# Thirteen chunks of the second layer's modulation, for the x stream alone, from TensorE in the first FFN pass to VectorE beside the mLSTM's projections

## The chip, the cores and the metric

One core of a Trainium2 chip runs the whole program. The metric is the device time of one execution in microseconds; lower is better. The kernel before took 2405.74 us (median of three runs, 2401.69 to 2405.82).

## What is computed

A two-layer block on an x stream of 1024 tokens (16 rows of 64) and a context stream of 256 tokens, 1024 features, all in float32. Per layer and stream a modulation vector of 6 x 1024 values is made from a conditioning vector, and used as shift, scale and gate:

```python
m = jax.nn.silu(cond) @ w + b            # w is 1024 x 6144
sh1, sc1, gt1, sh2, sc2, gt2 = split(m)
hx = rms_norm(x, g0) * (1 + sc1) + sh1   # then mixer: pooling (layer 0), mLSTM (layer 1)
x = x + gt1 * rms_norm(mixer(hx), g1)
x = x + gt2 * rms_norm(conv_ffn(modulate(x, g2, sh2, sc2)), g3)
```

The context stream goes through layer 0 in full; in layer 1 it only feeds the mLSTM's state, so of layer 1's modulation it needs sh1 and sc1 alone. The convolutional FFN has 2816 hidden features (22 tiles of 128), `silu(conv3x3(g)) * u`, and a projection back. The mLSTM projects hx and hc to q, k (which get a 3x3 convolution and silu), v, o and gates, and runs over chunks of 128 tokens in both directions.

## The kernel before

**Order of the work.** The program is written by hand, one instruction stream for each engine, with semaphores between them. Features lie on partitions, tokens on the free dimension. Its stages: pooling and layer 0's modulation; the FFN pass of layer 0 on x (22 tiles); the same FFN on the context (`ctx_ffn`); the mLSTM's projections (12 weight tiles, t = 0 to 11, in the order of `MSEQ`: o, qk, o, qk, o, qk, v, qk, v, v, v, o); the mLSTM's chunks; its output projection; the FFN pass of layer 1. Every float32 product is made of three products of high and low halves (`triple`).

**An FFN tile.** TensorE does seven products of four steps each (`products`, a Strassen-like scheme: g1, s1, s2, s4, s3, g2, u2) and then the 16 output products of the tile before (`down`), three matmuls to a step. VectorE does the eight convolution taps (`f_taps`), the sums between the products (`gate_second`, `up_second`, `gate_first_half`), the gating and the 16 additions into y (`f_add`). ScalarE and GpSimd split weights and activations into halves. In `products`, u2 waits for `up_second`; `down` waits for the gated halves, and for the additions three steps back.

**Layer 1's modulation** is cut into 24 chunks of 256 columns. Chunks 0 to 20 are done in the first FFN pass: chunk 0 before it, chunk j - 1 in tile j. There TensorE multiplies the conditioning vectors of both streams, padded to 32 columns (`c_pad`), with the weights of half a chunk in `modh`, in four matmuls of 256 columns (`first_rows`, L1222), once before g1 and once between s2 and s4. ScalarE copies the result to `mod_row` (`first_mod_in`), and in the next tile two matmuls (`first_columns`, L1229) turn it to columns, which ScalarE copies to `modt`. SyncE loads each half chunk (512 KB) between the weight loads (`first_mod_half`). Chunks 21 to 23 are made by VectorE for x alone in the second FFN pass (`last_mod_part`, L2678 and L2681: one multiplication, then seven multiply-adds of 256 columns into `macc_x`), and turned to columns by TensorE (`last_mod_columns`, L907: two matmuls of one column for each chunk). `derive` forms scale and gate factors from `modt`.

**The mLSTM's projections.** A qk tile makes two 128-feature blocks m (m = 0 to 7 over t = 1, 3, 5, 7): TensorE projects (`qk_tile`), ScalarE starts the convolution (`conv_first`), VectorE does its eight taps in place (`qtaps`, L3052), and for m = 4 to 7 two more on the context's part (L3060, counted by `kctap_done`). TensorE may write the next context part (from m = 5) only when the taps of the one before are done:

```python
if m >= 5:
    pe.wait_ge(sem("kctap_done"), 2 * (m - 4))
```

`vo_tile` projects a v or o tile, ScalarE evacuates it. After t = 8 `project_gates` follows, which waits for all taps; then `soft_gates` on ScalarE. VectorE also does two small scalings (`ctx_scale`) and the low half of the gates' weights (`lo_tile(K_GATE)`, before m = 6, L2651). GpSimd makes the low half of each weight tile in one instruction (`lo_tile`, L3338). SyncE loads tile t (1 MB, L586) when the low half of tile t - 2 is made; with tile 7 goes the gates' half (512 KB, L592).

Of the kernel before, what the change touches and what calls it, by code (L numbers as in the profile page):

```python
# [137 lines left out]
M = 2  # L138
MADE_FIRST = ("g1", "g2", "s1", "s2", "s4", "s3", "u2")
# [5 lines left out]
def build(nc, a):  # L145
    with ExitStack() as ctx:
# [6 lines left out]
                  "first_raw_in": "inc_in", "first_raw_out": "pmc_in"}  # L153
# [144 lines left out]
        mod_row = at("mod_row", EXT + 12288, [P, MODW])  # L298
        small = [SMALL]
# [266 lines left out]
        def _(sp):  # L566
# [58 lines left out]
            def the_rest():  # L625
# [25 lines left out]
                rows_done(M, 1)  # L651
                first_mod_half(M, 0)
                with sp.Fori(0, (FT - 2 - M) // 2) as i:
                    for e in range(2):
                        j = i * 2 + (M + 1 + e)
                        halves_in(i * 2 + (M + 2 + e))
# [3 lines left out]
                        rows_done(j, 1)  # L660
                        first_mod_half(j, 0)
# [3 lines left out]
                rows_done(FT - 1, 0)  # L665
                first_mod_half(FT - 2, 1)
# [122 lines left out]
            gates_in(len(units) - 1)  # L789
            sp.dma_start(f_raw[:], a["ffn_w"][FT][:, 0:2048]).then_inc(sem("raw_in0"), 16)  # L790
# [50 lines left out]
        def _(pe):  # L841
# [50 lines left out]
            def mod_columns(c):  # L892

                pe.wait_ge(sem("mod_sum"), c * 16 + 16)
                for b in range(2):
                    for x in range(2):
                        mm = pe.matmul(ps[:, 3, MODW + 2 * b + x:MODW + 2 * b + x + 1], macc[:, x, P * b:P * b + P], ones[:, 0:1],
                                       start=(b == 0 and x == 0), stop=(b == 1 and x == 1), skip_group_check=True)
                mm.then_inc(sem("modcol1_ready"), 1)
# [344 lines left out]
            def products(j, third=False, last=False):  # L1244
# [10 lines left out]
                if S.first and not third:  # L1255
                    pe.wait_ge(sem("dve_moved"), j * 3 + summed)
                    pe.wait_ge(sem("mod_sum"), j * 16 - 16)
                    first_columns()
                    first_rows(j, 0)
                if not third:  # L1260
                    product("g1", made("g1"))
                if last:
                    pe.wait_ge(sem("mod1_done"), FT)
# [10 lines left out]
                if S.first:  # L1274
# [4 lines left out]
                if S.first and not third:  # L1279
                    pe.wait_ge(sem("mod_sum"), j * 16)  # L1280
# [34 lines left out]
            with pe.Fori(0, (FT - 2 - M) // 2) as i:  # L1315
# [4 lines left out]
            products(FT - 1)  # L1320
            pe.wait_ge(sem("mod_sum"), 16 * (FT - 1))
            pe.wait_ge(sem("dve_moved"), 3 * FT + FIRST["dve_moved"])
            first_columns().then_inc(sem("modcol1_ready"), 1)
# [102 lines left out]
            def gate_columns():  # L1426

                pe.wait_ge(sem("gates_ready"), 2)
                for n in range(NCH):
# [9 lines left out]
            for t, (kind, i) in enumerate(MSEQ):  # L1439
# [4 lines left out]
                if t == T_SCAN:  # L1444
                    project_gates()
# [218 lines left out]
            for d in range(7):  # L1664
                paired(0, d, 1, False, True)
                if d == 3:
                    pe.wait_ge(sem("mod1_done"), FT)
# [23 lines left out]
        def _(act):  # L1691
# [136 lines left out]
            def last_mod_in():  # L1828

                act.wait_ge(sem("modcol1_ready"), M + 2)  # L1830
                for x in range(2):
                    ins = act.activation(modt[:, x, 2 * (FT - 1 + MODR):2 * (MODR + MODR)], ps[:, BANK_C, MODW:MODW + 6], ACT.Copy)
# [70 lines left out]
            def ctx_tile(j):  # L1903
# [3 lines left out]
                if j == 0:  # L1907
                    act.wait_ge(sem("mod_sum"), 16 * (FT - 1))
# [134 lines left out]
            def tile(j, par, gate_first=False, last=False, fourth=False):  # L2043
# [64 lines left out]
                if S.first:  # L2108
                    first_mod_in(j)
                if not last:  # L2110
# [112 lines left out]
            with act.Fori(0, (FT - 4 - M) // 2) as i:  # L2223
                tile(i * 2 + (M + 2), 0)
                tile(i * 2 + (M + 3), 1)
            tile(FT - 2, 0)
            tile(FT - 1, 1, last=True)
            act.wait_ge(sem("modcol1_ready"), M + 1)
            columns_in(FT - 2)
# [119 lines left out]
            for t, (kind, i) in enumerate(MSEQ):  # L2349
# [19 lines left out]
                else:  # L2369
                    if t == T_SCAN + 1:  # L2370
# [1312 lines left out]
```

## Time and profile before

| | |
|---|---|
| median of three runs | 2405.74 us (2401.69 to 2405.82) |
| profiled execution, its own time | 2407.11 us |
| its span, first to last instruction | 2405.3 us |
| TensorE busy with matmuls | 2301.6 us (96%), weight loads 1885.0 us (78%) |
| VectorE, ScalarE, GpSimd busy | 1567.4 us (65%), 929.3 us (39%), 1155.1 us (48%) |
| the chain that ended last, by engine | PE 82%, DVE 5%, POOL 4%, DMA 3%, issue 3%, ACT 2% |
| mean granted TensorE clock | 0.984 of 2.4 GHz |

PE is TensorE, DVE VectorE, ACT ScalarE, POOL GpSimd, SP SyncE. Times are microseconds from the start of the span. Each float32 matmul of the program shows as two in the trace ("x8" for four), and matmuls overlap, so the distance of two starts is the time that one takes, not its duration. A wait ("idle before", "<-") is put down to what came last.

### The profile page before, as it was taken

The numbers are of one execution on the slowest core, as the hardware profiler recorded it, in microseconds if no ns is written. First come the engines' busy times: TensorE is split into PE (matmuls) and PEld (weight loads), VectorE is DVE, ScalarE is ACT, GpSimd is POOL, SyncE is SP. The second block draws the span as 40 slices with busy tenths as digits, with TensorE's granted clock in tenths as the row PEclk, the third lists the DMA queues.
The fourth block names the chain that finished last, engine by engine and source line by source line (L and its number), as shares of the span: only waits on it lengthen the run. The fifth ranks groups of instructions, "written<-read, shape, count | busy, mean of one in ns | idle before, by whom it ended". The sixth has DMA issues, their size and how long they took to land.

```text
span 2405.3 us, 36943 instructions
## 1 busy us (share of the span) xinstructions
PE 2301.6 (96%) x13630; PEld 1885.0 (78%) x13630; DVE 1567.4 (65%) x2033; ACT 929.3 (39%) x1439; POOL 1155.1 (48%) x675
## 2 busy tenths in 40 slices
PE   7989999999999999999999998889989999999996
PEld 5457778777778778998899997767768888888884
DVE  4477577777777784552553406723768777889986
ACT  2553333333333345563342323333643333333332
POOL 0036566655555545662231005630586666666653
PEclk9999999999999999999999999999999999999998
DMA  8654322222222246552222138712211111112213
GB/s 340 241 201 174 107 75 75 76 87 87 87 80 85 85 159 229 195 183 88 71 72 74 53 117 229 218 53 71 70 53 53 52 52 52 52 61 70 70 44 140
DMA packets 112408, 263.57 MB, mean 110 GB/s; under 512 B 9392, under 2 KB 63280, under 8 KB 100016
## 3 DMA queue, kind: packets, MB, share of 16 engines
q1 hardware_dynamic: 94736, 236.95, 29.2%
q10 hardware_dynamic: 17568, 25.17, 2.9%
q8 instruction: 72, 1.18, 0.2%
q14 instruction: 32, 0.26, 0.0%
HBM read 227.88 MB, written 34.21 MB: 109 GB/s over the span
## 4 chain that ended last, share of the span: by engine, by line
PE 82%; DVE 5%; POOL 4%; DMA 3%; issue 3%; ACT 2%; SPq 0%; ACTq 0%; POOLq 0%; DVEq 0%
PE ps L844 11%; PE ps L846 10%; PE ps L845 10%; PE ps L1213 10%; PE ps L1215 10%; PE ps L1214 10%; PE ps L1343 2%; PE ps L1345 2%; PE ps L1344 2%; PE ps L1496 1%; PE ps L946 1%; PE ps L881 1%; PE ps L979 1%; DMA raw<-in_ffn_w 1%; PE ps L1222 1%
## 5 line engine op out<-in xcount | busy, mean ns | idle before, releaser
L2796 DVE TENSOR_TENSOR y_x<-y_x,ps 128x512 f32<-128x512 f32 x640 | 434.5, 688 | 89.2 <-PE ps L846 89.1
L2746 DVE SCALAR_TENSOR_TENSOR acc<-ps,fcv,acc 128x945 f32<-128x945 f32 (+2 forms) x336 | 410.6, 1222 | 35.9 <-DVE acc L2746 4.5
L3338 POOL TENSOR_TENSOR w_lo<-raw,w_hi 128x2048 fp32r<-128x2048 f32 x36 | 169.6, 4711 | 371.4 <-ACT w_hi L1815 251.2
L844 PE MATMUL ps<-fa_hi,fw_hi 128*128 128x512 f32 x672 | 265.7, 395 | 7.6 <-DVE acc L2746 4.2
L846 PE MATMUL ps<-fa_lo,fw_hi 128*128 128x512 f32 x672 | 263.3, 392 | 0.0
L845 PE MATMUL ps<-fa_hi,fw_lo 128*128 128x512 f32 x672 | 263.2, 392 | 0.0
L3396 POOL TENSOR_TENSOR p_g_lo<-f_raw,p_g_hi 128x512 fp32r<-128x512 f32 x80 | 104.0, 1301 | 326.3 <-ACT p_g_hi L1978 326.3
L3396 POOL TENSOR_TENSOR p_s_lo<-p_s_val,p_s_hi 128x512 fp32r<-128x512 f32 x160 | 210.7, 1327 | 32.7 <-ACT p_s_hi L1978 32.7
L2055 ACT ACTIVATE keep_a<-ps 128x512 f32<-128x512 f32 x40 | 23.9, 598 | 380.0 <-PE ps L1215 380.0
L844 PEld LDWEIGHTS ps<-fa_hi,fw_hi 128*128 128x128 f32 x672 | 127.0, 189 | 40.2 <-issue 5.0
L1343 PE MATMUL ps<-w_hi,hx_hi 128*128 128x256 f32 x512 | 146.0, 285 | 4.2 <-ACT stage L2299 4.1
L846 PEld LDWEIGHTS ps<-fa_lo,fw_hi 128*128 128x128 f32 x672 | 127.1, 189 | 26.9
L845 PEld LDWEIGHTS ps<-fa_hi,fw_lo 128*128 128x128 f32 x672 | 127.2, 189 | 25.6
L1344 PE MATMUL ps<-w_lo,hx_hi 128*128 128x256 f32 x512 | 145.6, 284 | 0.0
L1345 PE MATMUL ps<-w_hi,hx_lo 128*128 128x256 f32 x512 | 145.5, 284 | 0.0
L3407 POOL TENSOR_TENSOR fa_lo<-fprod,fa_hi 128x1024 fp32r<-128x1024 f32 x40 | 96.7, 2417 | 96.6 <-ACT fa_hi L2041 96.6
L1978 ACT ACTIVATE p_s_hi<-p_s_val 128x512 fp32r<-128x512 f32 x160 | 99.8, 624 | 80.2 <-POOL p_s_val L3387 80.0
L3052 DVE SCALAR_TENSOR_TENSOR acc_q<-ps,prm,acc_q 128x945 f32<-128x945 f32 (+2 forms) x64 | 78.2, 1222 | 69.2 <-ACT acc_q L2245 67.2
L3402 POOL TENSOR_TENSOR fw_lo<-fw_raw,fw_hi 128x1024 fp32r<-128x1024 f32 x42 | 101.3, 2411 | 34.5 <-ACT fw_hi L1990 34.4
L3387 POOL TENSOR_TENSOR p_s_val<-f_raw 128x512 f32<-128x512 f32 x80 | 105.1, 1314 | 5.8 <-DMA f_raw<-in_ffn_w 5.8
L1815 ACT ACTIVATE w_hi<-raw 128x2048 fp32r<-128x2048 f32 (+1 forms) x62 | 95.4, 1545 | 26.3 <-DMA raw<-in_mlstm_w 15.1
L1343 PEld LDWEIGHTS ps<-w_hi,hx_hi 128*128 128x128 f32 x512 | 98.9, 193 | 4.9 <-issue 2.7
(454 smaller groups left out, 6223.2 us busy)
## 6 DMA issues: line engine op xcount, KB each, us to landing
f_raw<-in_ffn_w SPq DMA_DIRECT2D x43, 1024.0 KB, 5.0
modw<-in_modw SPq DMA_DIRECT2D x48, 512.0 KB, 6.9
raw<-in_ffn_w SPq DMA_DIRECT2D x23, 1024.0 KB, 5.2
modh<-in_modw SPq DMA_DIRECT2D x46, 512.0 KB, 4.1
fw_raw<-in_ffn_w SPq DMA_DIRECT2D x42, 512.0 KB, 3.6
raw<-in_mlstm_w SPq DMA_DIRECT2D x14, 1024.0 KB, 5.3
raw<-in_ffn_w SPq DMA_DIRECT2D x24, 512.0 KB, 3.8
vch<-v_scr SPq DMA_DIRECT2D x18, 512.0 KB, 4.3
```

The lines of the kernel that those rows point to most:

```text
L844: pe.matmul(out, whi, hhi, start=first, stop=False)
L845: pe.matmul(out, wlo, hhi, start=False, stop=False)
L846: return pe.matmul(out, whi, hlo, start=False, stop=last)
L1213: pe.matmul(out, p_hi[p][:, ws], S.x(q, k)[0], start=(k == 0 and name in ("g1", "g2", "s1")), stop=False, skip_group_check=True)
L1214: pe.matmul(out, p_lo[p][:, ws], S.x(q, k)[0], start=False, stop=False, skip_group_check=True)
L1215: mm = pe.matmul(out, p_hi[p][:, ws], S.x(q, k)[1], start=False, stop=(k == KH - 1), skip_group_check=True)
L1343: pe.matmul(out, hi[:, k, t0:t0 + CH], wcol(0, k, 0, 2), start=first, stop=False)
L1344: pe.matmul(out, hi[:, k, t0:t0 + CH], wcol(1, k, 0, 2), start=False, stop=False)
L1345: return pe.matmul(out, lo[:, k, t0:t0 + CH], wcol(0, k, 0, 2), start=False, stop=last)
L2746: dve.scalar_tensor_tensor(out, src, cv[:, t:t + 1], out, ALU.mult, ALU.add).then_inc(sem("tap_done"), 1)
L2796: dve.tensor_tensor(y, y, ps[:, BANK_Y + n % 3, :], ALU.add).then_inc(sem("y_added"), 1)
L3396: pool.tensor_tensor(p_lo[p][:], src, p_hi[p][:].bitcast(F32), ALU.subtract).then_inc(S.sem("lo_in"), 1)
```

## The change

Two constants part the chunks: 0 to 7 stay in the first FFN pass (tiles 2 to 8), 8 to 20 become "late", 21 to 23 stay as they were. Tiles 9 to 21 of the first pass lose their `first_rows`, and 10 to 21 their columns, with ScalarE's copies and SyncE's loads; the loops of SP, PE and ACT are cut in two at tile 8. In the projections, SyncE loads the late chunks in halves behind the weight tiles 5, 7 and 9; VectorE makes them behind m = 1, 3 and 5 (4, 4 and 5 chunks); TensorE turns all 13 to columns ahead of `project_gates`, and ScalarE copies them out. VectorE's `derive` of the factors is split in two.

```diff
+EARLY, LATE = 8, 21
...
+        late_w = [at(f"late_w{h}", EXT + 4096 * h, [P, KH, MODW]) for h in range(2)]
...
+            def late_mod_in(c):
+                for h in range(2):
+                    if c > EARLY:
+                        sp.wait_ge(sem("mod_sum"), 16 * (c - 1) + 8 * (h + 1))
+                    sp.dma_start(late_w[h][:], a["modw1"][c][:, KH * h:KH * h + KH, :]).then_inc(sem(f"late_in{h}"), 16)
...
                 tile_in(K, a["mlstm_w"][t], K % 2)
                 if K == K_GATE:
                     tile_out(K, a["mlstm_w"][t], K % 2)
+                for c in {5: range(EARLY, EARLY + 4), 7: range(EARLY + 4, EARLY + 8), 9: range(EARLY + 8, LATE)}.get(t, ()):
+                    late_mod_in(c)
...
+            def late_mod_columns():
+                pe.wait_ge(sem("mod_sum"), 16 * LATE)
+                pe.wait_ge(sem("kctap_done"), 8)
+                for i in range(LATE - EARLY):
+                    for b in range(2):
+                        at_ = TC + 2 * i + b
+                        mm = pe.matmul(ps[:, 4, at_:at_ + 1], late_acc[i][:, P * b:P * b + P], ones[:, 0:1], ...
+                mm.then_inc(sem("modcol1_ready"), 1)
...
-                if S.first and not third:
+                if S.first and not third and columns:
                     pe.wait_ge(sem("dve_moved"), j * 3 + summed)
                     pe.wait_ge(sem("mod_sum"), j * 16 - 16)
-                    first_columns()
-                    first_rows(j, 0)
+                    mm = first_columns()
+                    if rows:
+                        first_rows(j, 0)
...
-                if S.first:
+                if S.first and rows:
                     first_rows(j, 1)
...
+            with pe.Fori(0, (FT - 4 - EARLY) // 2) as i:
+                products(i * 2 + (EARLY + 3), rows=False, columns=False)
+                down(i * 2 + (EARLY + 2), 0)
...
                 if t == T_SCAN:
+                    late_mod_columns()
                     project_gates()
...
+            def late_mod(c):
+                out = late_acc[c - EARLY][:]
+                for k in range(KT):
+                    if k % KH == 0:
+                        dve.wait_ge(sem(f"late_in{k // KH}"), 128 + 16 * (c - EARLY + 1))
+                    w = late_w[k // KH][:, k % KH, :]
+                    if k == 0:
+                        ins = dve.tensor_scalar(out, w, c_pad[:, 0, 0:1], None, ALU.mult)
+                    else:
+                        dve.wait_ge(sem("mod_sum"), c * 16 + 2 * k)
+                        ins = dve.scalar_tensor_tensor(out, w, c_pad[:, k, 0:1], out, ALU.mult, ALU.add)
+                    ins.then_inc(sem("mod_sum"), 2)
...
                 if m == 2:
                     ctx_scale(1, "c_pre1", 1, 0)
+                for c in {1: range(EARLY, EARLY + 4), 3: range(EARLY + 4, EARLY + 8), 5: range(EARLY + 8, LATE)}.get(m, ()):
+                    late_mod(c)
```

## Rows read from the trace of the kernel before

**Rows 1.** Windows: us, PE busy (x), granted clock, DMA share, GB/s.
```profile
303.00:845.00 542.00, 542.00 (x2580) 1.00 0.24 84
1093.00:1400.00 307.00, 302.79 (x2189) 0.99 0.22 76
```
**Rows 2.** Waits of the window 300 to 845: total us, times, longest.
```profile
DVE y_x L2796 <- PE ps L846: 46.0, 17, 2.7
```
**Rows 3.** Timeline of PE, first pass: start, us, instruction; tiles 20 and 21.
```profile
805.67 0.50 PE L1229 MATMUL ps<-fold,mod_row 128*128 128x2 f32 x4
806.10 0.64 PE L1222 MATMUL ps<-modh,c_pad 128*32 128x256 f32 x8
...
815.14 0.64 PE L1222 MATMUL ps<-modh,c_pad 128*32 128x256 f32 x8
...
847.10 0.64 PE L1222 MATMUL ps<-modh,c_pad 128*32 128x256 f32 x8
```
**Rows 4.** Timeline of DVE in the second pass, two tiles.
```profile
2130.23 0.70 DVE L2769 TENSOR_TENSOR ps<-keep_b,ps 128x512 f32<-128x512 f32 x1 [0.36 <-PE ps L1215]
...
2133.74 0.34 DVE L2678 TENSOR_SCALAR macc_x<-modh,c_pad 128x256 f32<-128x256 f32 x1
...
2160.27 0.70 DVE L2769 TENSOR_TENSOR ps<-keep_b,ps 128x512 f32<-128x512 f32 x1 [0.37 <-PE ps L1215]
...
2163.77 1.06 DVE L2681 SCALAR_TENSOR_TENSOR macc_x<-modh,c_pad,macc_x 128x256 f32<-128x256 f32 x2
```
**Rows 5.** Timeline of PE where three chunks are turned to columns.
```profile
2329.28 1.40 PE L907 MATMUL ps<-ones,macc_x 128*128 128x1 f32 x12
```
**Rows 6.** Timeline of DVE in the mLSTM's projections.
```profile
1189.38 10.02 DVE L3052 SCALAR_TENSOR_TENSOR acc_q<-ps,prm,acc_q 128x945 f32<-128x945 f32 x8 [3.27 <-ACT acc_q L2245]
...
1236.96 10.02 DVE L3052 SCALAR_TENSOR_TENSOR acc_q<-ps,prm,acc_q 128x945 f32<-128x945 f32 x8 [24.49 <-ACT acc_q L2245]
1246.90 0.99 DVE L3060 SCALAR_TENSOR_TENSOR acc_c<-ps,prm,acc_c 128x255 f32<-128x255 f32 x2
...
1261.59 1.22 DVE L2651 TENSOR_TENSOR w_lo<-raw,w_hi 128x1024 fp32r<-128x1024 f32 x1
1293.32 10.03 DVE L3052 SCALAR_TENSOR_TENSOR acc_q<-ps,prm,acc_q 128x945 f32<-128x945 f32 x8 [30.51 <-ACT acc_q L2245]
```
**Rows 7.** Timeline of SP: when the weights of tiles 5, 7 and 9 are issued.
```profile
1158.25 0.33 SPq L586 DMA_DIRECT2D raw<-in_mlstm_w  x1
...
1208.08 0.46 SPq L592 DMA_DIRECT2D raw<-in_mlstm_w  x1
...
1259.51 0.33 SPq L586 DMA_DIRECT2D raw<-in_mlstm_w  x1
```
**Rows 8.** DMA issues, KB each, median us to landing: windows 1085-1400, then 1726-1735.
```profile
raw<-in_mlstm_w SPq DMA_DIRECT2D x1, 512.0 KB, 6.2
...
modh<-in_modw SPq DMA_DIRECT2D x1, 512.0 KB, 3.7
```
**Rows 9.** Timelines of POOL and DVE, context FFN and projections, in order of time.
```profile
1040.17 1.21 POOL L3360 TENSOR_TENSOR ac_lo<-prod_c,ac_hi 128x256 fp32r<-128x256 f32 x1 [2.20 <-ACT ac_hi L1917]
...
1040.70 1.23 DVE L2844 SCALAR_TENSOR_TENSOR hx_lo<-y_x,modt,hx_hi 128x512 fp32r<-128x512 f32 x1
...
1092.54 6.54 DVE L2844 SCALAR_TENSOR_TENSOR hx_lo<-y_x,modt,hx_hi 128x512 fp32r<-128x512 f32 x9
...
1212.76 4.61 POOL L3504 TENSOR_TENSOR mc_lo<-y_c,mc_hi 128x2048 fp32r<-128x2048 f32 x1 [5.08 <-ACT mc_hi L2290]
...
1227.65 4.60 POOL L3338 TENSOR_TENSOR w_lo<-raw,w_hi 128x2048 fp32r<-128x2048 f32 x1 [10.28 <-ACT w_hi L1815]
```
**Rows 10.** Timeline of PE: the last projection step of m = 5.
```profile
1249.07 0.39 PE L846 MATMUL ps<-hx_lo,w_hi 128*128 128x512 f32 x1
```
**Rows 11.** Timeline of PE: the first instruction behind a stall in t = 0.
```profile
1110.78 0.36 PE L1343 MATMUL ps<-w_hi,hx_hi 128*128 128x256 f32 x1 [2.54 <-ACT stage L2299]
```
**Rows 12.** Window 1110 to 1115: us, PE busy (x), granted clock, DMA share, GB/s.
```profile
1110.00:1115.00 5.00, 4.22 (x23) 0.66 0.41 97
```

More of the change, by code:

```diff
@@ L298, in build @@
         mod_row = at("mod_row", EXT + 12288, [P, MODW])
+        late_w = [at(f"late_w{h}", EXT + 4096 * h, [P, KH, MODW]) for h in range(2)]
+        late_acc = [at(f"late_acc{i}", (RAW, W_HI, W_LO)[i // 4] + 8192 + 1024 * (i % 4), [P, MODW]) for i in range(12)] + [macc_x[0]]
         small = [SMALL]
@@ L659, in the_rest @@
                         first_mod_half(i * 2 + (M + e), 1)
-                        rows_done(j, 1)
-                        first_mod_half(j, 0)
+                with sp.Fori(0, (FT - 2 - EARLY) // 2) as i:
+                    for e in range(2):
+                        halves_in(i * 2 + (EARLY + 2 + e))
+                        out_in(i * 2 + (EARLY + e))
                 sp.wait_ge(sem("first_lo"), FIRST["lo_in"] + 7 * FT)
@@ L898, in mod_columns @@
                                        start=(b == 0 and x == 0), stop=(b == 1 and x == 1), skip_group_check=True)
+                mm.then_inc(sem("modcol1_ready"), 1)
[5 more added lines that the diff above has]
+                        at_ = TC + 2 * i + b
+                        mm = pe.matmul(ps[:, 4, at_:at_ + 1], late_acc[i][:, P * b:P * b + P], ones[:, 0:1],
+                                       start=(i == 0 and b == 0), stop=(i == LATE - EARLY - 1 and b == 1), skip_group_check=True)
                 mm.then_inc(sem("modcol1_ready"), 1)
@@ L1242, in third_first, with products @@
                     product(name, j * 7 + (S["lo_in"] + S.made_at(True, name)), True)
-            def products(j, third=False, last=False):
+            def products(j, third=False, last=False, rows=True, columns=True):
                 def made(name):
@@ L1278, in products @@
                 product("s3", made("s3"), third, low.get("s3"))
-                if S.first and not third:
-                    pe.wait_ge(sem("mod_sum"), j * 16)
+                if S.first and not third and columns:
+                    if rows:
+                        pe.wait_ge(sem("mod_sum"), j * 16)
                     pe.wait_ge(sem("mod1_done"), j - 1)
@@ L2041, in gated_high, with tile @@
                 act.activation(((fa_hi3 if S.first else fa_hi2) if last else fa_hi)[:], fprod[:, par, :], ACT.Copy).then_inc(sem("a_hi_ready"), 1)
-            def tile(j, par, gate_first=False, last=False, fourth=False):
+            def tile(j, par, gate_first=False, last=False, fourth=False, rows=True, columns=True):
                 def done(name):
@@ L2107, in tile @@
                 gate_moved_too()
-                if S.first:
+                if S.first and rows:
                     first_mod_in(j)
+                elif S.first and columns:
+                    act.wait_ge(sem("modcol1_ready"), M + 1)
+                    columns_in(EARLY - 1)
                 if not last:
@@ L2222, in _ @@
             tile(M + 1, 1, fourth=True)
-            with act.Fori(0, (FT - 4 - M) // 2) as i:
+            with act.Fori(0, (EARLY - M) // 2 - 1) as i:
                 tile(i * 2 + (M + 2), 0)
                 tile(i * 2 + (M + 3), 1)
[L2226 to L2229, printed above, removed]
+            tile(EARLY, 0)
+            tile(EARLY + 1, 1, rows=False)
+            with act.Fori(0, (FT - 3 - EARLY) // 2) as i:
+                tile(i * 2 + (EARLY + 2), 0, rows=False, columns=False)
+                tile(i * 2 + (EARLY + 3), 1, rows=False, columns=False)
+            tile(FT - 2, 0, rows=False, columns=False)
+            tile(FT - 1, 1, last=True, rows=False, columns=False)
             out_high(FT - 1, True)
@@ L3145, in _ @@
             own_done()
+            dve.wait_ge(sem("mod1_done"), EARLY + 1)
+            derive(1, (2, 3, 4), 6)
             dve.wait_ge(sem("gexp_in"), 2)
```

50 lines of the change are left out of this document (31 added, 19 removed).

## Prediction, written before the changed kernel was run

> **What bounds the kernel now.** I began with busy time by stage. In the first FFN pass TensorE is busy in all 542 us of its loop at full clock, in the projections in 302.8 of 307 us [rows 1]. The waits of the FFN window say the same from the other side: no wait of TensorE on another engine is among the long ones, while VectorE waits 2.7 us in each tile for the first output product [rows 2]. So in both stages a matmul taken out or put in counts in full, as long as VectorE and the queues keep up. Then I went through the timelines for the price of what moves, and for the room that VectorE has in the projections.
>
> **What goes.** From the second half of `first_rows` in tile 20 to that in tile 21 are 847.10 - 815.14 = 31.96 us [rows 3]. A tile of the second pass, with the same products, taps and additions and no rows, takes 2160.27 - 2130.23 = 30.04 us [rows 4]; VectorE has 0.36 us of room left there before `gate_second` and still does not set the pace. So rows and columns cost 1.92 us a tile, and 13 tiles lose them: 25.0 us. Tile 9 keeps its columns, 806.10 - 805.67 = 0.43 us [rows 3]. The last `first_columns`, behind tile 21, sits ahead of a wait for a load that starts at a fixed distance from g2: I give it nothing. Gain: **24.5 us**. It can't be more than 25.0; if VectorE, whose room shrinks by 1.9 us, is late by 0.3 us in each tile, it is 21. ScalarE's two copies and SyncE's two loads per tile go too; nothing waited for them, so 0.
>
> **What comes on TensorE.** Turning three chunks to columns is 12 passes in 1.40 us [rows 5], 0.117 us each. Thirteen chunks are 52 passes: **+6.1 us**, ahead of `project_gates`, where nothing hides it. The same row gives little spread, 5.5 to 6.7. ScalarE's two copies out of PSUM lie under the gates' products: 0.
>
> **What comes on VectorE.** Half a chunk is one multiplication of 0.34 us and three multiply-adds of 0.53 us (two take 1.06), the other half four multiply-adds [rows 4]: 1.93 + 2.12 = 4.05 us a chunk, 53 us in all. VectorE has the time: it sits idle 24.49 us before m = 4 and 30.51 us before m = 6 [rows 6]. But each half has one buffer. The next half-chunk is issued when the buffer is free and lands 3.7 us later when alone, 6.2 us later behind a 1 MB load [rows 8]. The half loads start about 2 us apart with nothing else large on the queues, so I take 3.7: a chunk comes every 1.93 + 3.7 = 5.63 us, of which VectorE waits 1.6. Four chunks take 3 x 5.63 + 4.05 = 20.9 us, five 26.6.
>
> Group by group, in the times of the trace before:
> - Behind m = 1: the first half is issued behind tile 5, at 1158.6 [rows 7], and lands at 1164.8. The end is 1185.7, ahead of the taps of m = 2 at 1189.38 [rows 6]: 0.
> - Behind m = 3: the loads stand behind tile 7 and the gates' half, which is issued at 1208.08 [rows 7] and lands at 1214.3; the first half comes about 1 us after that. GpSimd's `mc_lo` runs until 1217.4 [rows 9], see below, so I start there; the end is 1238.3, against 1236.96 for the taps of m = 4 [rows 6].
> - Behind m = 5: issued behind tile 9, at 1259.9 [rows 7], landed at 1266.1, end 1292.7. The low half of the gates' weights must follow (1.22 us [rows 6]): 1293.9, against 1293.32 for m = 6 [rows 6].
>
> **GpSimd's long instructions.** Each multiply-add reads two operands from SBUF. Such an instruction of 512 columns takes 0.73 us alone (nine in 6.54) and took 1.23 when it began 0.53 us into one of GpSimd of 1.21 us: it ended 0.55 us after that one's end [rows 9]. So VectorE seems to stand while GpSimd's instruction runs. One of 4.60 us lies in the second group (1227.65 [rows 9]) and, 56.36 us later by the distance of the rows of m = 4 and m = 6 [rows 6], one in the third. The 1.6 us in which VectorE would have waited for a load anyway come off: 3.0 us each. From below it is 0.5, what was seen once; from above the full 4.6. I take 3.0.
>
> The Trainium skill speaks against the change here: "SBUF — State Buffer", section "SBUF: two separate sides", says that a VectorE instruction with two SBUF inputs and a GpSimd instruction that reads SBUF exclude each other for a whole instruction. No row before shows it for an instruction as long as 4.6 us. Read strictly, without the waits taken off, it makes the two blocks 9.2 us where I have 6.0, and the total 3 us worse.
>
> With 3.0 us each the second group ends at 1241.3, 4.3 us late, the third at 1296.9, 3.6 us late. Who waits: TensorE may not write the context part of m = 5 before the two small taps of m = 4, which ended at 1247.9 [rows 6]; TensorE was there at 1249.07 + 0.23 = 1249.3 [rows 10]. Of each delay 1.4 us is free. Stalls: 2.9 and 2.2, **+5.1 us**. Both are at least near the 2.54 us behind which TensorE ran slow: in the 5 us from 1110 the granted clock was 0.66 [rows 11, 12], about 3.4 us at 1.2 instead of 2.4 GHz, 1.7 us lost. I count it once: **+1.7 us** (0 to 3.4; another 1.7 if 6 us of one-column matmuls have the same effect).
>
> **Queues.** SyncE issues tiles 6, 8 and 10 only behind the last late half of a group. The last issue of a group comes when VectorE has finished the chunk before the last, near 1236 and 1290; tiles 8 and 10 were issued near 1232 and 1289 and used 20 us later, so it is 0. On VectorE, m = 2, 4 and 6 and `lo_tile(K_GATE)` stand behind a group; the gates' half is needed only after t = 8: 0. The split `derive` and the wait of `gate_columns` for the copied columns lie where VectorE and ScalarE are done long before: 0.
>
> **Sum.** -24.5 + 6.1 + 5.1 + 1.7 = -11.6 us. The profiled execution took 2407.11, so 2395.5; the median of the runs, 2405.74, lies 1.4 lower and makes it 2394.1. I say **2394 us**. Bounds: best -25.0 + 5.5 + 0 = -19.5; worst of this case -21 + 6.7 + 9 + 3.4 = -1.9. What a measurement of this kernel can tell from no change is 0.2%, 4.8 us.
>
> **Rivals.**
> 1. *The late chunks are hidden.* GpSimd's instruction meets VectorE while it waits for loads anyway, so each block costs its lower end, and delays stay under about 1.5 us. For it: without the blocks the groups end 1.3 and 0.6 us late, as much as is free. Against it: the instruction of 1.21 us held VectorE to its end [rows 9]. Time: -24.5 + 6.1 + 0 to 1, about 2388. Chance 0.25.
> 2. *Each long GpSimd instruction holds VectorE for its full 4.6 us*, with nothing hidden by the loads' waits, and both stalls have their slow clock behind them. For it: the row of 1.21 us; against it: after such a hold both buffers are full, and the next load's wait falls away. With the stalls near their upper bounds: -24.5 + 6.1 + 9 + 3.4 + 1.7 = -4.3, 2401.4 from the median. This is what the Trainium skill's rule from above would give at its strictest. Chance 0.12.
> 3. *VectorE becomes the bound of the FFN pass.* Its room in front of the output product is 2.7 us [rows 2], but it isn't all in one place; if only 1.0 us a tile comes out, the sum is -13 + 6.1 + 6.8 = 0, 2406. Against it stands the tile of 30.04 us. Chance 0.07. That the change doesn't do what it says would look the same here.
> 4. *The loads set the pace*, slower than before. If a half takes 6.2 us to land each time, as behind 1 MB [rows 8], a chunk comes every 8.1 us, the second group ends 3 x 2.5 = 7.5 us later and the third 10 us later; stalls 5.1 + 17.5 = 22.6, clock 3.4: -24.5 + 6.1 + 22.6 + 3.4 = +7.6, 2413.3. It turns from gain to loss where a half takes about 5.1 us. For it: a single buffer per half, and ScalarE's output transfers in the same time. Against it: the 3.7 us, and a DMA share of 0.22 in the stage [rows 1]. Chance 0.08.
> My forecast keeps 0.48.
>
> **How the numbers follow.** Faster by over 0.2% (under 2400.9) are the forecast, rival 1 and half of rival 2: 0.79. Within 0.2% are the other half of rival 2 and rival 3: 0.13. Slower: rival 4, 0.08. The range must hold 8 in 10: from 2386.5, a little under rival 1, to 2403, beyond rival 2; rivals 3 and 4 and the tails stay out.
>
> **What would show it.** Right: first-pass tiles from 9 on of 30.0 us, a PE row of 52 one-column passes of about 6 us, two waits of TensorE of 2 to 4 us on VectorE's context taps in t = 5 and t = 7, late half loads of 3.7 to 4 us, multiply-adds of 0.47 us and one of several us beside each long GpSimd instruction. Wrong: tiles above 30.5 us; no waits in t = 5 and 7; late loads above 5 us; a wait of TensorE in t = 3 or at the gates' products.

## The result, and the profile after

The changed kernel took **2407.74 us** (median of 15 runs, 2404.74 to 2411.04); the kernel before, on the same chip, 2404.14 us (15 runs). The ratio is 1.0018, 95% interval 1.0011 to 1.0025: about 4 us slower, where 11.6 us of gain had been forecast. All times compared below are of fast runs; one of the 12 runs of i_ahead, of 3366.28 us, was slow and is left out. The profiled execution took 2411.04 us, its span is 2409.2 us, 3.9 us above that of before.

The page after, its sections on busy time and on the chain that ended last:

```profile
PE 2288.3 (95%) x13422; PEld 1885.6 (78%) x13422; DVE 1622.4 (67%) x2139; ACT 925.4 (38%) x1415; POOL 1154.9 (48%) x675
...
PE 74%; DVE 9%; DMA 6%; POOL 5%; issue 3%; ACT 2%; SPq 0%; ACTq 0%; DVEq 0%; POOLq 0%
```

TensorE is busy 13 us less, and its share of the last chain fell from 82 to 74%: VectorE and the DMA queues have come into that chain. Windows of PE (us, busy, granted clock, DMA share, GB/s), against [rows 1]:

```profile
1093.00:1400.00 307.00, 288.08 (x2017) 0.96 0.32 104
303.00:845.00 542.00, 539.04 (x2438) 1.00 0.20 68
```

The FFN loop is still full of TensorE; the projections have lost 15 us of it, and some of the clock. ScalarE's gated halves, one for each FFN tile, time the first stage; before:

```profile
309.95 1.06 ACT L2041 ACTIVATE fa_hi<-fprod 128x1024 fp32r<-128x1024 f32 x1 [2.43 <-DVE fprod L2754]
...
855.88 1.06 ACT L2041 ACTIVATE fa_hi<-fprod 128x1024 fp32r<-128x1024 f32 x1 [4.87 <-DVE fprod L2754]
```

and after:

```profile
307.93 1.06 ACT L2087 ACTIVATE fa_hi<-fprod 128x1024 fp32r<-128x1024 f32 x1 [2.43 <-DVE fprod L2807]
...
829.63 1.06 ACT L2087 ACTIVATE fa_hi<-fprod 128x1024 fp32r<-128x1024 f32 x1 [4.74 <-DVE fprod L2807]
```

Between the same two tiles, 17 apart, lie 545.93 us before and 521.70 after: the tiles gave 24.2 us. The tiles without rows are 30.04 us apart (from 466.70 to 797.12 there are 11). In the projections, ScalarE's first step on each pair of blocks is the marker. Before, m = 0, 2, 4, 6 and the gates:

```profile
1138.68 1.21 ACT L2245 ACTIVATE acc_q<-ps,prm 128x1024 f32<-128x1024 f32 x1 [0.81 <-PE ps L846]
...
1188.13 1.21 ACT L2245 ACTIVATE acc_q<-ps,prm 128x1024 f32<-128x1024 f32 x1 [0.81 <-PE ps L846]
...
1235.72 1.21 ACT L2245 ACTIVATE acc_q<-ps,prm 128x1024 f32<-128x1024 f32 x1 [8.15 <-PE ps L846]
...
1292.08 1.21 ACT L2245 ACTIVATE acc_q<-ps,prm 128x1024 f32<-128x1024 f32 x1 [8.15 <-PE ps L846]
...
1351.31 1.11 ACT L2318 ACTIVATE gates_x<-ps,prm 128x1024 f32<-128x1024 f32 x1 [11.02 <-PE ps L846]
```

After:

```profile
1111.38 1.21 ACT L2297 ACTIVATE acc_q<-ps,prm 128x1024 f32<-128x1024 f32 x1 [0.81 <-PE ps L861]
...
1161.54 1.21 ACT L2297 ACTIVATE acc_q<-ps,prm 128x1024 f32<-128x1024 f32 x1 [0.81 <-PE ps L861]
...
1209.34 1.21 ACT L2297 ACTIVATE acc_q<-ps,prm 128x1024 f32<-128x1024 f32 x1 [6.24 <-PE ps L861]
...
1275.30 1.21 ACT L2297 ACTIVATE acc_q<-ps,prm 128x1024 f32<-128x1024 f32 x1 [7.12 <-PE ps L861]
...
1355.12 1.11 ACT L2370 ACTIVATE gates_x<-ps,prm 128x1024 f32<-128x1024 f32 x1 [16.23 <-PE ps L861]
```

At m = 0 the changed kernel is 27.3 us ahead; at the gates it is 3.8 behind, and so it stays to the end. The whole of the result lies between m = 0 and the gates. Two stretches lose: m = 4 to 6 (56.36 became 65.96) and m = 6 to the gates (59.23 became 79.82). Waits of TensorE after, from 1040 to 1420 (total us, times, longest; the kernel before has no wait of TensorE on VectorE there):

```profile
PE ps L859 <- DVE acc_c L3113: 16.6, 2, 9.2
PE ps L1380 <- ACT stage L2351: 3.4, 2, 1.8
PE ps L871 <- ACT sq_c L1744: 0.6, 1, 0.6
```

The first line is the wait on the context's taps, 7.4 us in t = 5 and 9.2 in t = 7. VectorE's timeline of the second group and the start of the third shows why they are late (start, us, instruction, idle time before it):

```profile
1190.34 0.80 DVE L3130 TENSOR_SCALAR late_acc<-late_w,c_pad 128x256 f32<-128x256 f32 x1
1191.24 4.04 DVE L3133 SCALAR_TENSOR_TENSOR late_acc<-late_w,c_pad,late_acc 128x256 f32<-128x256 f32 x7
1196.83 0.35 DVE L3130 TENSOR_SCALAR late_acc<-late_w,c_pad 128x256 f32<-128x256 f32 x1 [1.55 <-DMA late_w<-in_modw]
...
1202.94 0.35 DVE L3130 TENSOR_SCALAR late_acc<-late_w,c_pad 128x256 f32<-128x256 f32 x1 [0.86 <-DMA late_w<-in_modw]
1203.40 8.22 DVE L3133 SCALAR_TENSOR_TENSOR late_acc<-late_w,c_pad,late_acc 128x256 f32<-128x256 f32 x7
1213.23 0.35 DVE L3130 TENSOR_SCALAR late_acc<-late_w,c_pad 128x256 f32<-128x256 f32 x1 [1.61 <-DMA late_w<-in_modw]
...
1217.37 2.25 DVE L3133 SCALAR_TENSOR_TENSOR late_acc<-late_w,c_pad,late_acc 128x256 f32<-128x256 f32 x4 [2.01 <-DMA late_w<-in_modw]
1219.54 10.02 DVE L3105 SCALAR_TENSOR_TENSOR acc_q<-ps,prm,acc_q 128x945 f32<-128x945 f32 x8
...
1251.13 0.35 DVE L3130 TENSOR_SCALAR late_acc<-late_w,c_pad 128x256 f32<-128x256 f32 x1 [9.82 <-DMA late_w<-in_modw]
```

GpSimd's instructions beside the first and the second group, and VectorE's last four multiply-adds of the first:

```profile
1160.80 4.77 POOL L3409 TENSOR_TENSOR w_lo<-raw,w_hi 128x2048 fp32r<-128x2048 f32 x1 [25.15 <-ACT w_hi L1854]
...
1203.18 4.60 POOL L3409 TENSOR_TENSOR w_lo<-raw,w_hi 128x2048 fp32r<-128x2048 f32 x1 [12.20 <-ACT w_hi L1854]
```
```profile
1160.62 6.41 DVE L3133 SCALAR_TENSOR_TENSOR late_acc<-late_w,c_pad,late_acc 128x256 f32<-128x256 f32 x4 [1.29 <-DMA late_w<-in_modw]
```

Seven multiply-adds take 4.05 us free and 8.22 beside GpSimd's instruction of 4.60 us at 1203.18; four take 2.25 free and 6.41 beside the one at 1160.80. The second group of four runs from 1190.34 to 1219.54, 29.2 us; the taps behind it could have started at 1210.6. The granted clock behind the two waits, and behind the run of one-column passes that ends at 1338 (PE windows, columns as above):

```profile
1225.00:1230.00 5.00, 0.00 (x0) 0.79 0.00 0
1230.00:1235.00 5.00, 4.48 (x22) 0.52 0.00 0
1290.00:1295.00 5.00, 0.00 (x0) 0.78 0.00 0
1295.00:1300.00 5.00, 1.77 (x8) 0.50 0.00 0
1300.00:1305.00 5.00, 5.00 (x33) 0.70 0.00 0
1338.00:1345.00 7.00, 7.00 (x21) 0.57 0.44 150
```

Behind both waits, and behind the run of passes, ahead of which it does not wait, TensorE works near 1.2 GHz for a few us (clock 0.50 to 0.57).

### The profile page after: what moved, and what is told of

Its sections match the earlier page's. It is cut to its first block, busy times and chain, and to the rows that moved or that the text cites. A ratio compares the mean times of both kernels' runs of the same rounds, so it can differ in the third digit from the quotient of the medians.

```text
span 2409.2 us, 36495 instructions
## 1 busy us (share of the span) xinstructions
PE 2288.3 (95%) x13422; PEld 1885.6 (78%) x13422; DVE 1622.4 (67%) x2139; ACT 925.4 (38%) x1415; POOL 1154.9 (48%) x675
## 3 DMA queue, kind: packets, MB, share of 16 engines
q1 hardware_dynamic: 94736, 236.95, 29.6%
## 4 chain that ended last, share of the span: by engine, by line
PE 74%; DVE 9%; DMA 6%; POOL 5%; issue 3%; ACT 2%; SPq 0%; ACTq 0%; DVEq 0%; POOLq 0%
PE ps L859 10%; PE ps L1239 10%; PE ps L1241 10%; PE ps L1240 10%; PE ps L861 9%; PE ps L860 9%; DMA late_w<-in_modw 2%; DVE acc_q L3105 2%; DVE late_acc L3133 2%; PE ps L1380 2%; PE ps L1382 1%; PE ps L1381 1%; PE ps L1535 1%; PE ps L972 1%; PE ps L1005 1%
## 5 line engine op out<-in xcount | busy, mean ns | idle before, releaser
L2101 ACT ACTIVATE keep_a<-ps 128x512 f32<-128x512 f32 x40 | 23.9, 598 | 359.5 <-PE ps L1241 359.5
L3458 POOL TENSOR_TENSOR p_s_val<-f_raw 128x512 f32<-128x512 f32 x80 | 105.2, 1315 | 5.7 <-DMA f_raw<-in_ffn_w 5.7
L859 PE MATMUL ps<-hc_hi,w_hi 128*128 128x256 f32 x352 | 100.2, 285 | 1.7 <-DMA hc_lo<-hc_scr 1.7
```

Of the source, the lines that this page charges most:

```text
L859: pe.matmul(out, whi, hhi, start=first, stop=False)
```

## The experiments

My theory after this reading: the late groups are too long for their gaps, because the halves of a chunk arrive too slowly in one buffer each and because GpSimd's long instruction holds VectorE for its whole length; slow clock comes on top. Rivals: VectorE's own work is already too much; the holds alone; something outside the groups, the columns above all.

All kernels are compared with the kernel before on the same chip (2403.8 us median in the first two sets, 2403.3 in the third), and by the distances of the same ScalarE markers in their profiles, in us. The distances are steadier than the rest of a profile. All 12 kernels with the change have the same instructions up to m = 0, and yet the first marker of an FFN tile, at 307.93 above, lies between 304.21 (j_four_spread) and 308.98 us (k_groups); and from the gates to the end the profiles take between 1052.10 (a_no_late) and 1058.15 us (b_loads_once). So a few us between two spans say nothing by themselves.

| kernel | m 0 to 2 | 2 to 4 | 4 to 6 | 6 to gates | sum | median us, ratio (95%) |
|---|---|---|---|---|---|---|
| before | 49.45 | 47.59 | 56.36 | 59.23 | 212.63 | 2404.14 |
| changed | 50.16 | 47.80 | 65.96 | 79.82 | 243.74 | 2407.74, 1.0018 (1.0011-1.0025) |
| a_no_late | 49.46 | 47.58 | 56.36 | 69.90 | 223.30 | 2388.13, 0.9937 (0.9924-0.9951) |
| b_loads_once | 49.46 | 47.59 | 56.79 | 69.92 | 223.76 | 2391.71, 0.9945 (0.9931-0.9958) |
| c_four | 50.60 | 48.86 | 57.28 | 69.90 | 226.64 | 2394.62, 0.9963 (0.9949-0.9976) |
| d_order | 50.41 | 47.59 | 59.59 | 75.76 | 233.35 | 2399.79, 0.9983 (0.9974-0.9992) |
| e_spread | 49.98 | 47.74 | 65.52 | 76.92 | 240.16 | 2406.44, 1.0017 (1.0005-1.0029) |
| i_ahead | 50.05 | 48.22 | 65.72 | 73.21 | 237.20 | 2402.70, 0.9996 (0.9986-1.0007) |
| g_all | 53.97 | 48.63 | 57.46 | 65.24 | 225.30 | 2392.21, 0.9955 (0.9942-0.9968) |
| h_all_ahead | 53.31 | 47.60 | 57.37 | 65.23 | 223.51 | 2392.08, 0.9961 (0.9945-0.9976) |
| j_four_spread | 55.26 | 48.72 | 57.24 | 65.23 | 226.45 | 2390.93, 0.9948 (0.9935-0.9961) |
| k_groups | 49.46 | 47.60 | 56.81 | 65.23 | 219.10 | 2387.20, 0.9929 (0.9915-0.9943) |
| l_groups_order | 49.46 | 47.60 | 56.56 | 65.24 | 218.86 | 2385.13, 0.9924 (0.9911-0.9938) |

**a_no_late**

```diff
-                for c in {5: range(EARLY, EARLY + 4), 7: range(EARLY + 4, EARLY + 8), 9: range(EARLY + 8, LATE)}.get(t, ()):
+                for c in ():
...
+                dve.memset(late_acc[c - EARLY][:], 0.0).then_inc(sem("mod_sum"), 16)
```

> Leaves out the 13 late chunks: each accumulator is only set to zero, nothing of them is loaded; the 52 one-column passes stay. What it times is the gain of the FFN pass and the columns. My theory (the late groups on VectorE cost what is missing): the context taps of m = 4 and m = 6 start early, neither long wait of TensorE on them is left, so against before -27.3 (FFN) +0.9 +6.3 (columns) +1 to 3 (their slow clock) = about -17 to -20 us, ratio 0.992 to 0.993. Rival A (the slow clock behind the columns or something else outside the groups is the main part): it stays above -10 us.

Measured: -15.7 us. Both long waits are gone, so all of them came from the late groups. The stage up to m = 6 is that of before to 0.02 us. But the stretch to the gates is 10.67 us longer, with 52 one-column passes that were priced at 6.1. It missed the expected range, -17 to -20, for two reasons. The expectation had 8.2 to 10.2 us for that stretch and for the first group; and its -27.3 for all that comes ahead of m = 0 holds 2.0 us by which the profile of before is later already at its first marker, inside the scatter named above. The two terms between markers, -24.2 and -1.05 (see the table of terms below), with +10.67 make -14.6. Its PE windows show the rest of the columns:

```profile
1308.00:1315.00 7.00, 7.00 (x49) 0.73 0.06 20
1315.00:1320.00 5.00, 5.00 (x16) 0.50 0.61 208
```

TensorE has no wait there at all, and still falls to 1.2 GHz during the run of one-column passes (1308.2 to 1316.3) and stays there behind it.

**b_loads_once**

```diff
-                for c in {5: range(EARLY, EARLY + 4), 7: range(EARLY + 4, EARLY + 8), 9: range(EARLY + 8, LATE)}.get(t, ()):
+                for c in {5: (EARLY,)}.get(t, ()):
...
-                        dve.wait_ge(sem(f"late_in{k // KH}"), 128 + 16 * (c - EARLY + 1))
+                        dve.wait_ge(sem(f"late_in{k // KH}"), 128 + 16)
```

> Loads only the first late chunk and uses its two halves for all 13, so 12 chunks are computed from wrong weights; VectorE's 104 instructions and GpSimd's long instructions stay as they are, the pace of the loads is gone. Theory L (the single buffers and landings of 4.3 us or more are the main part): the second group ends near 1190.3 + 4 x 4.4 + 4.6 = 1212.5, its stall falls from 7.4 to about 1 us, the third from 9.2 to about 3 or less; against before -11 to -15 us. Theory V (VectorE's own work of 4.4 us a chunk, with GpSimd's holds, is already too much): both stalls stay above 5 us and the total between -4 and +2 us.

Measured: -12.1 us, and 0.46 us more than without late chunks between m = 0 and the gates, though VectorE does all 104 instructions. In its second group it is even held twice (seven multiply-adds take 8.39 and 8.29 us, from 1182.66 and 1195.84), and the taps are on time but for 0.2 us; its third group ends at 1253.50, ahead of GpSimd's instruction at 1254.27. The rival "VectorE's own work is too much" is out. The row of its multiply-adds:

```profile
L3133 DVE SCALAR_TENSOR_TENSOR late_acc<-late_w,c_pad,late_acc x84: 483/485/4818, 1136.4 to 1248.7; 128x256 f32<-128x256 f32 x84
```

(Minimum, median and maximum in ns.) So holds of 4.8 us cost TensorE next to nothing (one wait of 0.2 us), once the loads do not also delay the group. The time is 3.6 us above that of a_no_late, where the stretch gives 0.46; the intervals overlap, and the rest is not explained.

**c_four**

```diff
-        late_w = [at(f"late_w{h}", EXT + 4096 * h, [P, KH, MODW]) for h in range(2)]
+        late_w = [at(f"late_w{h}", (EXT, EXT + 4096, Y_AT + 24576, Y_AT + 28672)[h], [P, KH, MODW]) for h in range(4)]
...
+                    n = 2 * (c - EARLY) + h
+                    if n >= 4:
+                        sp.wait_ge(sem("mod_sum"), 16 * (c - 2) + 8 * (h + 1))
```

> Four half-chunk buffers in place of two; the loads run up to two chunks ahead of VectorE. Theory L: VectorE's waits on late loads (35 us in 19 times) fall below 12 us and lie at the starts of the groups; both stalls fall to 0 to 4 us; -9 to -15 us against before. Theory V: stalls above 5 us, -4 to +2 us. If the landing time grows as much as the depth (the queues are the limit, not the latency), the waits stay near 30 us and the time near +2.

Measured: -9.2 us. No wait of TensorE on the taps is left. VectorE's waits on late loads, from 1080 to 1345, in the changed kernel

```profile
DVE late_acc L3130 <- DMA late_w<-in_modw: 24.0, 10, 9.8
DVE late_acc L3133 <- DMA late_w<-in_modw: 9.1, 7, 2.0
```

and with four buffers

```profile
DVE late_acc L3132 <- DMA late_w<-in_modw: 13.0, 3, 6.3
```

are one for each group's first half. A half lands in 6.0 us (median) instead of 4.3, and it does not matter inside a group: the depth hides it. That answers the expectation's third case; the queues are not the limit inside a group.

**d_order**

```diff
+                if t in (4, 6, 8):
+                    pool.wait_ge(sem("mod_sum"), {4: 16 * (EARLY + 4), 6: 16 * (EARLY + 8), 8: 16 * LATE}[t])
                 lo_tile(K_MIN + t)
```

> GpSimd's low part of the weights of t = 4, 6 and 8 starts only when the late group before it is done, so no GpSimd instruction of 4.6 us runs beside a late group; loads as in the changed kernel. Theory T (loads, holds and clock together): the multiply-add of 4.66 us is gone from the maximum of its row (under 1.5 us), the second group ends about 4 us earlier and the third about 3; stalls from 16.6 to about 9 us; -3 to -5 us against before. Theory H (the holds are the main part): stalls under 3 us, -10 us or better. If GpSimd, put off by up to 8 us, is needed by TensorE, new waits of TensorE on GpSimd's parts appear in t = 5 and 7 and the time is over before.

Measured: -4.0 us, as theory T had it. The longest multiply-add is 0.488 us:

```profile
L3133 DVE SCALAR_TENSOR_TENSOR late_acc<-late_w,c_pad,late_acc x84: 483/485/488, 1138.6 to 1268.8; 128x256 f32<-128x256 f32 x84
```

The two waits shrink from 16.6 to 8.0 us (3.0 and 5.0). So without the holds half of the waiting is left, and without the waits for loads (b_loads_once) 0.2 us: the loads are the larger part. Either cure takes away more than what it alone had added, since both lengthen the same groups and TensorE feels only what goes beyond the slack.

**e_spread**

```diff
-                    late_mod_columns()
                     project_gates()
...
+                        if part < 2 and k < 7 and 7 * part + k < LATE - EARLY:
+                            late_mod_columns(7 * part + k, 7 * part + k + 1)
```

> As the changed kernel, but two of the one-column matmuls (four passes) stand behind each of 13 k-steps of the gates' products instead of all 52 passes in one run. The run with the late chunks left out has 69.90 us from the acc_q copy of m = 6 to the gates' copy where the kernel before has 59.23: 10.67 for columns that I priced at 6.1, with a granted clock of 0.56 in 1310 to 1320. If the run of one-column passes is what TensorE turns slow behind, that stretch falls to 65.5 to 66.5 us and the time by 3 to 4 us, to about 0 against before; if passes of one column cost that wherever they stand, it stays at 69 to 70 and the time at +4. The stalls stay at 16 us in both cases.

Measured: 2.7 us above before (1.0017), the time of the changed kernel within the intervals, so the expected 3 to 4 us are not seen in the time. In the profile the stretch to the gates is 76.92 us instead of 79.82, 2.9 us less and not the expected 65.5 to 66.5, for it still holds a stall of 8.7 us and its slow clock: the expectation had kept the stalls and left them out of its stretch. The clean comparison is between kernels without stalls: 69.90 to 69.92 us in a, b and c, 65.23 to 65.24 us in g, h, j, k and l, which all have the spread form; c_four and j_four_spread differ in nothing else. That is 4.7 us, and 6.0 above the kernel before: what the passes cost at full clock. The window of the last kernel below, over the same time as a_no_late's above:

```profile
1308.00:1315.00 7.00, 7.00 (x47) 1.00 0.07 24
1315.00:1320.00 5.00, 5.00 (x32) 1.00 0.45 136
```

**i_ahead**

```diff
+                first = {7: EARLY + 4, 9: EARLY + 8}.get(t)
+                if first:
+                    for c in range(first, first + 1):
+                        late_mod_in(c)
                 tile_in(K, a["mlstm_w"][t], K % 2)
...
-                for c in {5: range(EARLY, EARLY + 4), 7: range(EARLY + 4, EARLY + 8), 9: range(EARLY + 8, LATE)}.get(t, ()):
+                for c in {5: range(EARLY, EARLY + 4), 7: range(EARLY + 5, EARLY + 8), 9: range(EARLY + 9, LATE)}.get(t, ()):
```

> As the changed kernel, but the first chunk of the second and third late group is issued ahead of the 1 MB weight tile of t = 7 and t = 9 instead of behind it. Theory: the first half of the third group landed 8.1 us after its issue behind that tile and VectorE had waited 9.8 us for it, so its group starts 8 to 10 us earlier and its stall of 9.2 us shrinks to 0 to 2; the second group starts behind GpSimd's instruction near 1190 anyway, so its 7.4 us lose 0 to 2. Against before -5 to -8 us. Rival (the pace inside the group decides, not its start): both stalls lose under 2 us each, time 0 to +3. A delay of the weight tiles by 1 MB would show as new waits of TensorE in t = 7 or 9; none expected.

Measured: 1.1 us below before with an interval of the ratio that holds 1, some 5 us better than the changed kernel. The expectation's sum against before was too good; the waits show what was right: 11.2 us in two, 7.8 us in t = 5, as much as before, and 3.3 in t = 7, down from 9.2 but not to 0 to 2. The place in SyncE's queue was worth 6 us of the third group's delay.

**g_all and h_all_ahead**

Buffers, order and spread columns together; h also issues the first two chunks of the second and third group ahead of the weight tiles.

> Four half-chunk buffers, GpSimd's low parts of t = 4, 6 and 8 behind the late groups, and the one-column matmuls spread over the gates' products. With four buffers alone: -9.2 us, no long wait on the taps left, but still 3.3 us more from m = 0 to the gates than with the chunks left out, and 10.7 for the columns. If these are the holds by GpSimd and the slow clock: -9.2 -2 to -3 -3 to -4 = -14.5 to -16.5 us. If putting GpSimd off costs TensorE as much as the holds did VectorE: -9 to -12.

> The same with the first two chunks of the second and third late group issued ahead of the weight tiles of t = 7 and 9. If the start of a group still costs something in the kernel with four buffers (VectorE waits 13 us in 3 times for the first chunks), it is 1 to 2 us better than without, about -17; if nothing waits there, the same within 1 us. A queue that then holds the weight tile too long would make it worse, with waits of TensorE or GpSimd on raw_in in t = 7.

Measured: -11.6 and -11.7 us. g_all is at the end of its range that stood for a costly order, and issuing loads ahead gave nothing, the second case of h_all_ahead's expectation. Up to the gates they lose 4.5 and 3.9 us between m = 0 and m = 2, behind the first group, where the changed kernel had lost 0.7. I blamed the order (GpSimd put off in t = 4) and tested that.

**j_four_spread**: as g_all without the order.

> Four half-chunk buffers and the spread one-column matmuls, GpSimd's order as in the changed kernel. It tells whether putting GpSimd off helped or hurt: with it, m = 0 to m = 2 took 53.97 us where the other kernels have 49.5 to 50.6, with a new wait of 3.0 us of TensorE on sq_c. If that order is what cost it, this stretch is 50.5 us here, m = 2 to the gates 171.5, and m = 0 to the gates 222 against 225.3 with the order: about -12 to -14 us against before. If not, 225 and -10 as with the order.

Measured: 55.26 us from m = 0 to m = 2, more than with the order. My reason was wrong, though the time, -12.4 us, lies in the range that I had tied to it: the hit is luck. TensorE waits 3.0 us on ScalarE's squares of the context (`sq_c`), and ScalarE waits for its own output transfers (ScalarE's longest wait from 1110 to 1165):

```profile
ACT stage L2355 <- DMA o_scr<-stage: 12.8, 4, 4.9
```

The transfers in that stretch (KB each, median us to landing):

```profile
late_w<-in_modw SPq DMA_DIRECT2D x8, 512.0 KB, 6.5
o_scr<-stage ACTq DMA_DIRECT2D x8, 128.0 KB, 5.3
```

And its PE windows:

```profile
1130.00:1140.00 10.00, 10.00 (x86) 1.00 1.00 369
1145.00:1150.00 5.00, 2.03 (x15) 0.88 0.57 202
1150.00:1155.00 5.00, 5.00 (x33) 0.50 0.01 2
```

Tile 5 (1 MB), then four half-chunks at once, fill the DMA engines from 1130 to 1140 (share 1.00), and ScalarE's 128 KB transfers, which land in 1.8 us without late loads, take 5.3. Behind the wait the clock is at its lower level once more. c_four is the same program up to the gates and loses 1.15 us there, not 5.8. In it the transfers land in 4.5 us, ScalarE's last wait for them is 3.2 us instead of 4.9, TensorE waits 1.1 us instead of 3.0, and its granted clock stays at 1.00 from 1145 to 1160. So of the difference of 4.7 us 1.9 are a longer wait and about 2.8 the slow clock; why the same transfers took longer in one execution is open.

**k_groups and l_groups_order**: groups of 3, 4, 5 and 1 chunks (the part of the edit on VectorE; SyncE's ranges follow it).

```diff
-                for c in {1: range(EARLY, EARLY + 4), 3: range(EARLY + 4, EARLY + 8), 5: range(EARLY + 8, LATE)}.get(m, ()):
+                for c in {1: range(EARLY, EARLY + 3), 3: range(EARLY + 3, EARLY + 7), 5: range(EARLY + 7, EARLY + 12), 7: range(EARLY + 12, LATE)}.get(m, ()):
```

> Four buffers, spread columns, the first two chunks of a group issued ahead of the weight tiles of t = 7 and 9, GpSimd's order as in the changed kernel, and groups of 3, 4, 5 and 1 chunks behind m = 1, 3, 5 and 7 in place of 4, 4, 5. The first group then leaves m = 2 alone: m = 0 to m = 2 falls from 50.6 to 49.5 us, the others stay at 47.6 to 49 and 56.4 to 57.3, m = 6 to the gates 65.2, in sum 219 to 221 us where the kernel before has 212.6 and the changed one 243.7. Against before -15 to -19 us. If the chunk behind m = 7 makes the columns late, the last stretch grows above 66.5 and the gain stays near -12.

> The same, with GpSimd's low parts of t = 6 and 8 (not of t = 4) behind the late groups. If the two holds still make the taps of m = 4 and m = 6 late, it is 1 to 2.5 us better than without the order; if the buffers and the early loads already cover them, it is the same within 0.5 us in the stretch from m = 2 to the gates; if TensorE then waits for GpSimd or what ScalarE makes of it, as it did for t = 4, that stretch is longer by 1 to 4 us.

Measured: -16.1 and -18.2 us; from m = 0 to the gates 219.10 and 218.86, both as expected (for the second, the case of the same stretch within 0.5 us). With three chunks in the first group, m = 0 to m = 2 takes 49.46 in both, what it takes without any late chunk, where four chunks took from 50.60 to 55.26 with four buffers; ScalarE's transfers land in 3.2 us in k_groups:

```profile
late_w<-in_modw SPq DMA_DIRECT2D x6, 512.0 KB, 8.0
o_scr<-stage ACTq DMA_DIRECT2D x8, 128.0 KB, 3.2
```

The order is worth 0.24 us between m = 2 and the gates; the 2.1 us between the two medians are no more than the intervals allow for chance. **l_groups_order has the lowest median**, 0.76% under the kernel before (0.62 to 0.89%). TensorE's longest waits in it, 1040 to 1420:

```profile
PE ps L1387 <- ACT stage L2359: 3.5, 2, 1.9
PE ps L1508 <- ACT stage L2359: 1.3, 1, 1.3
```

The others are under 1 us. None is on the taps or on a late chunk.

## Why the prediction was wrong

The mechanism and its places were right, the sign of the time was not. Term by term, by the profiles:

| term | predicted | measured |
|---|---|---|
| FFN tiles | -24.5 | -24.2 |
| ahead of and behind these tiles | 0 | -3.1 |
| one-column passes | +6.1 | +6.0 (spread form) |
| stalls at the context's taps | +5.1 | +16.6 (7.4 and 9.2) |
| slow clock | +1.7 | +7.6 |
| first group and rest, m = 0 to 4 | 0 | +0.9 |
| sum | -11.6 | +3.8 |

The clock term is what the two stretches hold beyond their stall and the passes: 9.60 - 7.44 = 2.2 and 20.59 - 9.19 - 6.0 = 5.4. The -3.1 is the 2.02 us by which the profile of before lies behind already at 309.95, where the change has not acted, and 1.05 between the marker of the last of these tiles and m = 0. Both can be scatter: the 12 changed kernels have the same instructions there and spread over 4.8 us at the first marker, and from it to m = 0 over 2.7 us (801.1 in a_no_late to 803.8 in i_ahead). That the sum meets the +3.9 of the spans shows only that the profiles are read in full; the medians give +3.6.

**The failing step is the length of a group**, in "What comes on VectorE". I had 20.9 + 3.0 = 23.9 us for the second and 29.6 for the third; they took 29.2 and 35.0. In the second:
- *The chunk itself*: 4.05 us by instruction times, 4.42 from start to start where nothing waits (in c_four one chunk starts at 1138.11, the next at 1142.53). I had halved the 1.06 us of two multiply-adds [rows 4], but 1.06 is one step and one duration: at 0.485 us each, seven in 4.05 us start 0.59 us apart, not 0.53. And I had given the multiplication its duration, not the 0.46 us to the next start. 4 x 0.37 = +1.5.
- *The loads*: I had 1.58 us of waiting between chunks, 4.7 in all; the rows above and those left out of them give 1.55 + 0.87 + 0.86 + 1.61 + 2.01 = 6.9. I had taken the landing of 3.7 us of a transfer alone [rows 8]; the median was 4.3. +2.2.
- *GpSimd's hold*: 8.22 - 4.05 = 4.2, and 0.45 at the start of the group, where `mc_lo` still ran; I had 3.0: +1.6. I had subtracted 1.6 us of load waits that were to fall away behind the hold. They did not: the waits right behind it are 1.61 and 2.01 us. Here the hold fell on the first multiply-add of a chunk, and a buffer is refilled only after VectorE, held too, has used it. In the third group the hold fell behind the chunk's first half, and there the first wait behind it is gone (the multiplication at 1273.67 has none) and the second is 1.80. The multiplication is held like the multiply-adds: 0.80 us at 1190.34, and 1.70 in c_four at 1188.62, where GpSimd's `mc_lo` ran until 1190.17.

Together 5.3, less 0.7 for an earlier start: 2.9 became 7.4. In the third group the same three give 5.4 by its length, and its first half landed 8.1 us after its issue at 1243.03 instead of 6.2, +1.9: 2.2 became 9.2. The first group was too short in the sum as well, 28.5 us instead of 20.9, and by that ran into a hold that I had not counted, the one of 6.41 us for four multiply-adds: the taps of m = 2 began 4.7 us late. TensorE did not feel it: the 0.7 us between m = 0 and m = 2 are its wait of 0.6 us on ScalarE's squares (`sq_c`). I had asked only whether each term was near its bound, not that all of them point the same way: once the 1.4 us of slack are gone, each us of a group is a us of TensorE.

**The clock** was counted once, with "0 to 3.4" beside it. It came after both stalls, and a third time with the one-column passes, where TensorE never waits: I had named that as a possible 1.7 us, it is 4.7 by itself in a_no_late. In the changed kernel it is less: full PE windows at 0.72 from 1335 to 1340 and at 0.60 from 1340 to 1345, by my estimate 5 x 0.28 + 5 x 0.40 = 3.4 us. Nor does a wait of about 3 us always bring it: behind that of 3.0 us in t = 5 of d_order the granted clock stayed at 1.00 (1225 to 1235), behind that of 3.0 us in j_four_spread it fell to 0.50.

**The rule of the Trainium skill** ("SBUF — State Buffer", section "SBUF: two separate sides") that I weighed against the row of 1.21 us: that a VectorE instruction with two SBUF inputs and a GpSimd instruction reading SBUF exclude each other for a whole instruction. Here the traces agree: a multiply-add of 0.485 us takes 4.66 us beside GpSimd's (4.82 in b_loads_once), and 0.488 at most where none runs beside it (d_order). Its strict reading, 9.2 us for the two blocks, was nearer than my 6.0: they measure 4.2 + 0.45 and 4.2.

**The rivals.** Rival 4 (loads set the pace) had the mechanism that costs most, but not its size: I put the turning point at a landing of 5.1 us for a half, and with 4.3 the kernel was already slower, since the full holds of rival 2 and three spells of slow clock came with it. b_loads_once shows that the holds alone are hidden (in the second group; its third met none); d_order that the loads alone still stall TensorE for 8.0 us. Each rival had one cause with the others at my central values; the result is both together. Rival 3 is out: 30.04 us a tile. Rival 1, the late chunks hidden, did not hold for this kernel; c_four, with four buffers, comes near to it.

## What to carry to other kernels

Where work is moved into another engine's gaps, compare each group's length with its gap: start-to-start times from a row, loads at the landing they have under the traffic of that stage, holds in full; and when the slack is about 1 us and the gap ends in TensorE's wait, add up the upper bounds, since past the slack they all count, and slow clock on top. Give such a stream of loads a second pair of buffers before judging the idea: it turned +4 us into -9. Here a run of 52 one-column passes cost 10.7 us, and 6.0 when spread between full matmuls.

## What the runs showed that I had not expected

- TensorE's granted clock fell to 1.2 GHz during an unbroken run of 52 one-column passes with no wait before it (0.73 in 1308 to 1315, 0.50 in 1315 to 1320 in a_no_late): 4.7 us. With four passes behind each step of the gates' products the clock stayed at 1.00.
- 512 KB loads queued four deep from SyncE slowed ScalarE's 128 KB transfers from 1.8 to 5.3 us (DMA share 1.00), and TensorE then stopped for 3.0 us, two engines away from the change. In c_four, the same program up to the gates, TensorE stopped for 1.1 us: a delay of this kind differs from execution to execution.
- The 4.7 us that the spread columns give without stalls are 2.9 in the profile of e_spread, where the passes had less to give (3.4 us, above). In the time they are 0.9 (2.7 against 3.6 us above before), with an interval 6 us wide: whether 2.9 or nothing was gained there, the runs can't tell.
